# A two-layer diffusion backbone on one core: raw weights in three places instead of four, split weights in four instead of three, and the first modulation in smaller stages

## What is computed

```python
def trunk_layer(l, x, cond, ...):
    mod = jax.nn.silu(cond) @ w_ada[l] + b_ada[l]
    shift, scale, gate = jnp.split(mod[:, None, :], 3, axis=-1)
    h = rmsnorm(x, norm_pre[l]) * (1 + scale) + shift
    proj = h @ w_in[l]                                   # 2048 x 5120
    if l % 2 == 0:
        q, k, v, g_a, u_b, g_b = jnp.split(proj, EVEN_SPLITS, axis=-1)
        ...
    else:
        u_c, g_c, u_d, v_d, g_d = jnp.split(proj, ODD_SPLITS, axis=-1)
        ...
    x = x + gate * rmsnorm(o @ w_out[l], norm_post[l])   # 2048 x 2048
```

## Time and profile before

| | us |
|---|---|
| median of 3 runs (1203.51 to 1207.18) | 1205.12 |
| the profiled execution | 1205.11 |
| its span | 1203.3 |
| opening, from the first step to the first of chunk 3 | 150.9 |
| PE busy | 1136.3 (94%) |
| DVE busy | 694.0 (58%) |
| ACT busy | 421.5 (35%) |
| POOL busy | 50.9 (4%) |

### The profile page before, as it was taken

One profiled execution on the slowest core, in us unless ns is written; L12 is line 12 of the kernel. 1 busy time (PEld: TensorE's weight loads), 2 busy tenths in 40 slices (PEclk: granted clock), 3 DMA queues, 4 the chain that ended last, 5 costly groups with the idle time before them and its releaser, 6 DMA issues.

```text
span 1203.3 us, 13779 instructions
## 1 busy us (share of the span) xinstructions
PE 1136.3 (94%) x5404; PEld 876.3 (73%) x5404; DVE 694.0 (58%) x949; ACT 421.5 (35%) x653; POOL 50.9 (4%) x98
## 2 busy tenths in 40 slices
PE   3799999999999999999999699999999999999994
PEld 0456677877787877777777388888788878878883
DVE  3354555678788784688873553466665643243333
ACT  3323234333455342233332673223233323242331
POOL 1000010000000001011111000000000000000000
PEclk9999999999999999999999799999999999999998
DMA  9998974655565576666678534444344633433413
GB/s 329 328 315 295 301 253 151 227 202 196 180 245 210 183 263 245 210 215 222 221 241 310 226 106 146 150 158 161 125 173 171 209 114 131 140 105 107 138 35 105
DMA packets 113056, 235.97 MB, mean 196 GB/s; under 512 B 5280, under 2 KB 38080, under 8 KB 109408
## 3 DMA queue, kind: packets, MB, share of 16 engines
q1 hardware_dynamic: 100976, 190.86, 46.1%
q0 software_dynamic: 11440, 41.08, 10.3%
q10 hardware_dynamic: 576, 3.16, 0.7%
HBM read 231.40 MB, written 3.67 MB: 195 GB/s over the span
## 4 chain that ended last, share of the span: by engine, by line
PE 82%; DMA 7%; DVE 6%; issue 2%; ACT 2%; SPq 0%; DVEq 0%; ACTq 0%
PE bank L732 23%; PE bank L734 22%; PE bank L733 22%; DMA wide_raw<-in_w_ada 5%; PE bank L754 3%; DVE wide L1313 2%; DVE w_lo L1147 2%; PE bank L856 1%; DVE x L1194 1%; PE bank L693 1%; DMA raw_first<-in_w_ada 1%; PE bank L839 1%; DMA raw<-in_w_in 1%; PE bank L901 1%; PE bank L800 1%
## 5 line engine op out<-in xcount | busy, mean ns | idle before, releaser
L732 PE MATMUL bank<-w_hi,h_op 128*128 128x512 f32 x1152 | 474.7, 412 | 7.2 <-DVE h_op L1358 4.2
L734 PE MATMUL bank<-w_hi,h_op 128*128 128x512 f32 x1152 | 452.9, 393 | 0.0
L733 PE MATMUL bank<-w_lo,h_op 128*128 128x512 f32 x1152 | 451.6, 392 | 0.0
L1147 DVE TENSOR_TENSOR w_lo<-raw,w_hi 128x1024 fp32r<-128x1024 f32 x224 | 272.9, 1221 | 196.6 <-ACT w_hi L938 196.3
L938 ACT ACTIVATE w_hi<-raw 128x1024 fp32r<-128x1024 f32 x224 | 234.7, 1054 | 244.5 <-PE bank L734 233.0
L732 PEld LDWEIGHTS bank<-w_hi,h_op 128*128 128x128 f32 x1152 | 217.8, 189 | 87.3 <-issue 40.5
L734 PEld LDWEIGHTS bank<-w_hi,h_op 128*128 128x128 f32 x1152 | 217.5, 189 | 48.6
L733 PEld LDWEIGHTS bank<-w_lo,h_op 128*128 128x128 f32 x1152 | 218.2, 189 | 40.5 <-issue 0.7
L1313 DVE SCALAR_TENSOR_TENSOR wide<-wide_raw,cond,wide 128x1024 f32<-128x1024 f32 x120 | 152.3, 1276 | 20.0 <-DMA wide_raw<-in_w_ada 19.8
L732 PE MATMUL bank<-w_hi,o_low 128*128 128x512 f32 x192 | 76.9, 400 | 3.1 <-DVE w_lo L1147 3.0
L734 PE MATMUL bank<-w_hi,o_low 128*128 128x512 f32 x192 | 74.9, 390 | 0.0
(11 more groups left out here) (181 smaller groups left out, 755.6 us busy)
## 6 DMA issues: line engine op xcount, KB each, us to landing
raw<-in_w_in SPq DMA_DIRECT2D x80, 1024.0 KB, 6.7
raw_first<-in_w_ada SPq DMA_DIRECT2D x64, 512.0 KB, 6.2
raw<-in_w_ada SPq DMA_DIRECT2D x32, 1024.0 KB, 5.7
wide_raw<-in_w_ada POOLq DMA_DIRECT2D x64, 512.0 KB, 4.3
raw<-in_w_out SPq DMA_DIRECT2D x32, 1024.0 KB, 5.1
x<-in_x_sample SPq DMA_DIRECT2D x2, 1024.0 KB, 9.7
x<-in_x_sample ACTq DMA_DIRECT2D x2, 1024.0 KB, 11.4
out_y_sample<-x SPq DMA_DIRECT2D x8, 256.0 KB, 3.1
```

The lines of the kernel that those rows point to most:

```text
L732: pe.matmul(out, operand(layer, kind, 0, k, t), hi, start=k % group == 0, stop=False)
L733: pe.matmul(out, operand(layer, kind, 0, k, t), lo, start=False, stop=False)
L734: last = pe.matmul(out, operand(layer, kind, 1, k, t), hi, start=False, stop=k % group == group - 1)
L1147: dve.tensor_tensor(w_lo[:, half % WRING, :, :].rearrange("p k n -> p (k n)"), src, hi, ALU.subtract)\
```

## The change

It does four things.

1. `RAW` goes from 4 to 3 and `WRING` from 3 to 4 (the same bytes in SBUF). Halves are split three halves ahead instead of two, and quarters stand in the list of loads one half earlier.
2. The opening: the first two stages have one slice each and 2 entries of 8 row slices (rows of 512 B), the other seven as before. Weights of chunks 0 to 2 are loaded by halves (512 KB) instead of quarters. The order of steps and spills changes (9 spills of 3 banks for 8), each stage of two slices now has its work in a fixed pattern of 6 steps, and ACT's table for the square root is loaded by an extra small operation ahead of its use.
3. The second set of wide sums starts 6 steps earlier (step 13 of chunk 8) with 1.1 steps between sums instead of 1; the first set goes from 1.3 to 1.2 steps.
4. At the seam 2 rows are PE products instead of 6, and the sums of layer 1 are 14 loads instead of 10, with 2.25 steps between sums instead of 2.5.

```diff
-SEAM_ADA = 6
+SEAM_ADA = 2
 ...
-WRING = 3
-RAW = 4
+WRING = 4
+RAW = 3
 FIRST_RAW = 3
 ...
-STAGES = 8
-WIDE = [(GATE_BLOCK[0], FIRST, 10, 13, 10), (SHIFT_BLOCK, FIRST + 6, 3, 1, 1)]
+WIDE = [(GATE_BLOCK[0], FIRST, 10, 12, 10), (SHIFT_BLOCK, FIRST + 5, 13, 11, 10)]
 ...
+STAGES = [[0], [1]] + [[2 * r, 2 * r + 1] for r in range(1, ROUNDS)]
+STAGE_OF = {k: b for b, ks in enumerate(STAGES) for k in ks}
+ENTRIES = [2 * len(ks) for ks in STAGES]
+def round_order(r):
+    return (2, 0, 1) if r % 2 == 0 else (1, 0, 2)
+OPENING = [(2, 0), (0, 0), (2, 1), (0, 1), (1, 0), (1, 1)]
+OPENING += [(c, 2 * r + i) for r in range(1, ROUNDS) for c in round_order(r) for i in range(2)]
 ...
     pre(0, "square")
-    for i in range(4):
-        pre(0, "first_ada", 0, i)
-        if i == 1:
-            pre(0, "norm")
-    pre(0, "first_weights")
+    pre(0, "norm")
+    pre(0, "first_ada", 0, 0)
+    pre(0, "norm_rest")
+    pre(0, "first_ada", 0, 1)
     pre(0, "first_cols", 0)
-    for k in range(2):
-        pre(0, "h", 0, k)
+    pre(0, "first_weights", 0)
+    pre(0, "h", 0, 0)
+    pre(0, "first_weights", 1)
+    pre(0, "first_ada", 1, 0)
+    first(0, "first_ada", 1, 1)
+    first(1, "first_cols", 1)
+    first(1, "h", 0, 1)
+    first(1, "first_weights", 2)
 ...
+    for b in range(3, len(STAGES)):
+        at_ = 6 * (b - 2)
         for i in range(4):
-            first(at_ + ada[i], "first_ada", b, i)
-        first(at_ + cols, "first_cols", b)
-        for k in range(2 * b, 2 * b + 2):
-            first(at_ + h, "h", 0, k)
+            first(at_ - 1 + i, "first_ada", b, i)
+        first(at_ + 3, "first_cols", b)
+        for k in STAGES[b]:
+            first(at_ + 4, "h", 0, k)
 ...
-                put(L1 + 1, 5 * n // 2, "lane_sum", half, i, j // 2, j % 2)
+                put(L1 + 1, 9 * n // 4, "lane_sum", half, i, j // 2, j % 2)
 ...
+    def opening_loads():
+        yield from (("first_ada", 0, 0), ("first_ada", 0, 1), ("mm", 0), ("mm", 1))
+        yield from (("first_ada", 1, 0), ("first_ada", 1, 1), ("mm", 2))
 ...
+            n = NTH_HALF[p[1], p[2] // 2] + 3
+            if n < len(HALVES) and NTH_UNIT[HALVES[n]] == fetched:
+                loads.append(("mm", fetched))
 ...
-                half = NTH_HALF[p[1], p[2] // 2] + 2
+                half = NTH_HALF[p[1], p[2] // 2] + WRING - 1
 ...
+                    if layer == 0 and t == 0:
+                        act.wait_ge(x_squared, 1)
+                        act.activation(junk[:, 0:1], stat[:, 4, 0:1], ACT.Sqrt)
```

More of the change, by code:

```diff
@@ L86 @@
 KEPT, SPILLED = 0, (1, 2)
[L87 to L89 removed]
+ROUNDS = KT // 2
+STAGES = [[0], [1]] + [[2 * r, 2 * r + 1] for r in range(1, ROUNDS)]
[5 more added lines that the diff above has]
+OPENING += [(c, 2 * r + i) for r in range(1, ROUNDS) for c in round_order(r) for i in range(2)]
+HALVES = [(c, r) for r in range(ROUNDS) for c in round_order(r)]
 HALVES += [(c, h) for c in range(FIRST, len(CHUNKS)) for h in range(KT // 2)]
 NTH_HALF = {ch: n for n, ch in enumerate(HALVES)}
[L92 to L96, removed]
+UNITS = [[(c, h)] for c, h in HALVES if c < FIRST]
+UNITS += [[(c, h), (c, h + 1)] for c, h in HALVES if c >= FIRST and h % 2 == 0]
+NTH_UNIT = {ch: n for n, unit in enumerate(UNITS) for ch in unit}
+STAYS = []
+for c_, k_ in OPENING:
+    if c_ in SPILLED:
+        if STAYS and STAYS[-1][0] == c_:
+            STAYS[-1][2] = k_
+        else:
+            STAYS.append([c_, k_, k_])
+NTH_STAY = {(c, k): n for n, (c, a, b) in enumerate(STAYS) for k in range(a, b + 1)}
 def bank_set(c):
@@ L180, in timetable @@
             for t in range(TOKS):
-                put(FIRST - 1, 12 + t, "evac", c, t)
+                put(FIRST - 1, 14 + t // 2, "evac", c, t)
             continue
         if c == SPILLED[0]:
[L185 to L188, removed]
+            first(-4, "evac", c, 1)
+            first(-3, "turn", c, 0)
+            first(-2, "evac", c, 2)
+            first(-2, "turn", c, 1)
+            put(FIRST, 0, "turn", c, 2)
             continue
@@ L250, in places @@
     yield ("pre", 0)
[L251 to L254, removed]
+    for c, s in OPENING:
+        yield ("at", c, s)
+    for c in range(FIRST, len(CHUNKS)):
+        yield ("pre", c)
+        for s in range(KT):
             yield ("at", c, s)
@@ L266, in hybrid_step @@
     assert len(nth_side) == len(side)
-    loads, fetched = [], 2
+    def opening_loads():
+        yield from (("first_ada", 0, 0), ("first_ada", 0, 1), ("mm", 0), ("mm", 1))
+        yield from (("first_ada", 1, 0), ("first_ada", 1, 1), ("mm", 2))
+        yield from (("first_ada", 2, 0), ("first_ada", 2, 1), ("mm", 3), ("first_ada", 2, 2), ("first_ada", 2, 3))
+        yield from (("mm", 4), ("mm", 5), ("first_ada", 3, 0))
+        for b in range(3, len(STAGES)):
+            for i in range(1, 4):
+                yield ("mm", 3 * (b - 1) + i - 1)
+                yield ("first_ada", b, i)
+            if b + 1 < len(STAGES):
+                yield ("first_ada", b + 1, 0)
+    loads = list(opening_loads())
+    fetched = 3 * ROUNDS
     for p in places():
         if p[0] == "at" and p[2] % 2 == 0:
[L273 to L278, removed]
+            n = NTH_HALF[p[1], p[2] // 2] + 3
+            if n < len(HALVES) and NTH_UNIT[HALVES[n]] == fetched:
+                loads.append(("mm", fetched))
+                fetched += 1
         for e in table.get(p, ()):
[L280 to L283, removed]
             if e[0] == "ada":
@@ L287, in hybrid_step @@
                 loads.append(("sum", e[1], e[2]))
-    assert [x[1] for x in loads if x[0] == "mm"] == list(range(len(QUARTERS)))
+    assert [x[1] for x in loads if x[0] == "mm"] == list(range(len(UNITS)))
+    assert [x for x in loads if x[0] == "first_ada"] == [e for e in side if e[0] == "first_ada"]
     nth_first = {x: n for n, x in enumerate(x for x in loads if x[0] == "first_ada")}
@@ L565, in _ @@
                     if old[0] == "mm":
-                        c, quarter = QUARTERS[old[1]]
-                        sp.wait_ge(lo_ready, max(NTH_HALF[c, 2 * quarter + i] for i in range(2)) + 1)
+                        sp.wait_ge(lo_ready, NTH_HALF[UNITS[old[1]][-1]] + 1)
                     elif old[0] == "sum":
@@ L1510, in part @@
                     norm_x(0)
-                    for j in range(PIECES):
+                    norm_piece(0)
+                elif what == "norm_rest":
+                    for j in range(1, PIECES):
                         norm_piece(j)
```

136 lines of the change are left out of this document (70 added, 66 removed).

## The result

The changed kernel takes 1214.92 us in the median (1214.24 to 1217.70) beside 1204.32 (1200.76 to 1207.18) of the kernel before on the same chip: a ratio of 1.0094, 95% interval 1.0062 to 1.0126. It is slower by about 10 us, where 12 us less was forecast and 1203 was the upper end of the range.

A forecast was written before the change was run, and what follows sets the result against it. PE, busy 94% of the span, was taken as the bound. Opening -9.0, output of layer 0 -9.0 and three places +5.9 gave -12.1 from 1205.11: 1193.0 us, range 1184 to 1203.

The forecast's parts named there:

- second half of the part on three places: Quarters behind ada pairs: PE loses 1.0 at two places, elsewhere only if L (issue to landing) exceeds 6.25 us.
- now they go out one by one: Quarter loads: argument against a 7.2 us landing time, since earlier loads were issued in twos and threes.
- The first half: Ada pairs, chunks 3 to 9: second load late at four of eight pairs, 3.2 us lost.
- the same formula: Second ada loads at four pairs: 4 x (2.9 + L - 7.3), with L, issue to landing, taken as 5.2 us.
- Three places bind: Rival: quarters' median landing time of 7.2 us makes the three-places term 25.6, total 1212.7 us; chance 0.08.
- The opening: Chunks 0 to 2: step 0 near 29 us instead of 36, step 6 at 53.7, in all -9.0 us.
- the price of short rows: First two opening stages: 1 MB in 2048 rows of 512 B takes 3.56 us, bounds 3.00 and 6.00.
- The pace: Opening stages: a 0.72 us wait for ACT to free the side bank goes in three stages, 2.2 us saved.
- The output of layer 0: Chunks 10 to 13: sparser wide sums stop DVE's split coming late, -9.0 us; other bound -4.5.
- the rival of sums that still bind: Rival, output of layer 0: half of the 9 us stays, total 1197.5 us; chance 0.12.
- Halves as single DMAs: Rival, opening: 512 KB loads at 4.2 us each with no fixed part hidden, 23 us more, 1216; chance 0.03.
- The seam: Between layers: four fewer rows on PE gain nothing, as PE waits there for DVE's residual and norm.

The follow-up runs named there:

- one_by_one: Changed kernel, but from chunk 3 SyncE waits for each load of a quarter or ada row to land before issuing the next: 1221.89 us.
- wide_only: Kernel before with only the new rhythm of the wide sums: 1193.50 us.
- rings_back: Changed kernel with the rings of before (four places of raw, three of split halves, quarters issued two halves ahead): 1193.11 us.
- entry_first: Changed kernel with the rings of before, and in the opening's load list each raw_first entry ahead of the half it stood behind: 1189.47 us.
- ada_singly: Changed kernel with the sixteen ada rows of layer 0's scale block taken one every 7 steps instead of two every 14: 1195.68 us.

## Why the prediction was wrong

**The step that failed** is the second half of the part on three places: that behind a pair "ACT waits in its list, not PE", that PE feels it at two places only, 1.0 each, and "elsewhere from L = 6.25". ACT waits behind every pair of chunks 3 to 8: 1.5 to 4.7 us where the load landed in 5.0 to 5.8 us, well under 6.25, and 5.3 and 15.7 where it took 8.2 and 8.1. PE follows through `qk_t`, `probs_t` and DVE's `mixed` and `o_low`, because attention's small operations stand in ACT's list right behind the rounding. The prediction looked at one copy in chunk 4, beside a pair behind which PE lost nothing (ACT waits 1.50 us there), and took it for all. Measured: about 12 us where 2.0 stood. The slow clock behind PE's longest waits, which the prediction said it had not seen and gave no price, is 1.3 of these 12, 1.1 of the 8.2 below, and 2.0 beside both. The argument that "now they go out one by one" was wrong as well: behind seven pairs three quarters went out together, since SyncE could not pass the first of them.

**The first half** of that part had the right mechanism and the right four places, and a size too small: 8.2 us where 3.2 stood. The second load of those pairs took 5.9, 6.4, 5.8 and 5.2 us where 5.2 was taken. The 0.2 us added for a wide transfer beside them was too little for three of the four; with their mean of 5.84 the same formula gives 4 x 1.44 = 5.8, beside 6.5 of waits in the rows. Of the rest 1.1 is the clock in chunk 9.

**The rival that won, and why it is not confirmed.** "Three places bind" gave 1212.7, against 1212.4 of span and 1214.92 of time, and 25.6 for a term that measured 24.3. Its reason was a landing time of 7.2 us. one_by_one speaks against that: with quarters at 5.1 us in the median the loss is 27. But the load in chunk 3 stayed as slow as before (8.3 us), and in the changed kernel the second loads of the four pairs, at 5.84 for 5.2, are worth 2.6 us by the formula. The price was right by accident.

**The opening** was right to step 0, and in the price of short rows. It failed in what follows: a wait of 2.7 us for DVE, which had a split ahead of the add, was not in the walk, and the late last entry was counted for one stage where it came in six. Step 6 started at 55.5 where 53.7 was forecast, 1.8 us late, and the other 2.9 us were lost behind it. The pace did lose its three waits of 0.72 us for ACT, the 2.2 us of the forecast, but the waits for entries took their place. By totals the new opening, the seam and layer 1 together are worth 0.4 us beside wide_only (1193.50 to 1193.11), with the entry put ahead 4.0. In the two profiles rings_back is 3.8 us ahead of wide_only at the start of chunk 3 and loses 1.3 of it in chunks 3 to 9 and 2.1 from chunk 14 to the start of chunk 27.

**The output of layer 0** was right in size, 9.1 for 9.0, with chunks 11 and 12 at 34. The reason given was the rhythm, with the longer reach as a help; the runs show that each alone suffices for these two chunks, so the rival of sums that still bind was wrong.

**Halves as single DMAs** fell too. Chunks 0 to 2 moved 304 GB/s with weights in 512 KB pieces, and in entry_first 318 at a DMA share of 0.96, against 291 at 0.88 before with weights in 1 MB pieces: 331 for each full share in both. The 4.2 us that this rival took for 512 KB alone is the median of the wide loads, which go over GpSimd's queue and not SyncE's. The rule of 1 MiB for each DMA in the Trainium skill, "DMA: Bandwidth & Descriptors", section "Bandwidth", does not show where the queue is kept full.

**The seam** and layer 1 came out 1.9 us shorter to the start of chunk 27, where 0.7 longer was forecast. The seam itself gave nothing, as forecast.

What stays open: ACT's wait is seen to reach PE in the rows, and PE's loss falls away in ada_singly and rings_back, where ACT's waits in chunks 3 to 7 are gone. No kernel was made in which ACT alone was freed of the wait with three places and pairs kept. How the 22 us would divide in the kernel before, with its own opening, was not tried.

## What to carry to other kernels

- When a ring loses a place, count what holds places for long: a block of two items in a ring of three leaves one place for everything else, and the queue that issues in order stops there. Taking the two items singly won back 20 of 24 us without a byte of memory.
- A wait in an in-order engine that is 35% busy is not free. Follow the instructions behind the waiting one to the engine that sets the time, at each place where the pattern occurs, not at one of them.
- A wait of PE of some microseconds can have a price behind it too, in steps at the slower clock: 2.7 us became 5.9 in chunk 9. Behind one of 2.5 us in chunk 7 the granted clock stayed at 1.00.
- Look at the first of a group of loads and not at the median: the median of a group issued together says how long the group is.

## What the runs showed of the hardware

- Three 1 MB loads issued on one queue from 289.51 to 290.99 us landed 5.2, 7.5 and 9.6 us after their own issues; the first was nearly as early as one alone (5.0 to 5.1). In other groups the third took up to 12.5. In one_by_one, where each waits for the one before it, chunks 3 to 9 took 350.1 us in place of 347.2.
- 1 MB on SyncE's queue beside two 512 KB loads and one of 256 KB on GpSimd's took 8.3 us in place of 5.1.
- 1 MB in 2048 rows of 512 B took 3.45 us (between two entries at the start of the program, at 16.69 and 20.14 us), where 1024 rows of 1 KB took 3.00.
